# Linear attention in slots between the projection's tiles, in one decoder step

## The reference, cut to what matters

```
h = rmsnorm(x, norm1_g) * (1 + sc1) + sh1          # sc1, sh1, ... from c @ w_ada
q_a, k_a, v_a, g_lr, r_a, q_d, k_d, v_d = split_proj(h @ w_in)
log_a = log_sigmoid(g_lr @ w_gate_up + b_gate) / 16
# per token and head:  S_t = diag(exp(log_a_t)) S_{t-1} + k_t^T v_t ,  o_t = q_t S_t
# evaluated in chunks: b = cumsum(log_a) inside the chunk
att   = sum_k q * k * exp(b_t - b_s), causal
o     = att @ v + (q * exp(b)) @ S
S_new = exp(b_last) * S + (k * exp(b_last - b))^T @ v
o_a = rmsnorm(o, gla_norm_g) * silu(r_a)
# then: dilated softmax attention of q_d, k_d, v_d in 12 heads, output projection, MoE
```

## Time and profile before

| | us |
|---|---|
| runs, median (lowest to highest) | 1424.47 (1423.12 to 1428.05) |
| the profiled execution's own time | 1426.68 |
| its span, first to last instruction | 1425.1 |
| PE busy | 1141.1 (80%) |
| DVE busy | 699.1 (49%) |
| ACT busy | 579.0 (41%) |
| POOL busy | 127.0 (9%) |

### The profile page before, as it was taken

How to read it: one execution, slowest core, us unless ns; L and a number is a source line. 1 busy time by engine, 2 the same in 40 slices (tenths; PEclk the granted TensorE clock), 3 DMA queues, 4 the chain that set the end, 5 groups by cost and what they waited for, 6 DMA issues and landing times.

```text
span 1425.1 us, 18556 instructions
## 1 busy us (share of the span) xinstructions
PE 1141.1 (80%) x6899; PEld 639.2 (45%) x6900; DVE 699.1 (49%) x1029; ACT 579.0 (41%) x850; POOL 127.0 (9%) x135
## 2 busy tenths in 40 slices
PE   3799579549898989898779995029899999999810
PEld 0355256436566666665444453014445544444400
DVE  2434334344435454544733335428765686656557
ACT  2222324133535353535531113027755566555433
POOL 0000001000000000000010000522111111111032
PEclk9899789759999999999798998559999999999955
DMA  9763200062313232383142440068977797779255
GB/s 344 282 227 142 54 0 0 9 167 55 100 49 90 60 90 60 90 295 103 47 121 68 140 163 31 0 236 321 381 267 261 290 373 276 284 257 368 103 189 182
DMA packets 122341, 234.43 MB, mean 164 GB/s; under 512 B 11079, under 2 KB 54569, under 8 KB 119200
## 3 DMA queue, kind: packets, MB, share of 16 engines
q1 hardware_dynamic: 111760, 200.37, 41.3%
q0 software_dynamic: 7200, 21.06, 4.0%
q10 hardware_dynamic: 3312, 12.06, 2.1%
HBM read 197.60 MB, written 35.64 MB: 164 GB/s over the span
## 4 chain that ended last, share of the span: by engine, by line
PE 63%; DVE 13%; DMA 10%; ACT 5%; issue 5%; POOL 2%; SPq 1%; DVEq 0%; POOLq 0%; ACTq 0%
PE banks L1576 7%; PE banks L1577 6%; PE banks L1578 6%; PE banks L1915 5%; PE banks L1917 5%; PE banks L1916 5%; PE banks L1737 3%; DMA arena<-in_moe_w_gate_dram 3%; PE banks L1751 2%; PE banks L1765 2%; DVE arena L1237 2%; PE banks L1934 2%; PE banks L1936 2%; PE banks L1935 2%; PE banks L1856 2%
## 5 line engine op out<-in xcount | busy, mean ns | idle before, releaser
L1469 DVE SCALAR_TENSOR_TENSOR arena<-arena 128x2048 f16<-128x2048 f32 x96 | 217.5, 2287 | 80.8 <-ACT arena L959 80.7
L959 ACT ACTIVATE arena<-arena 128x2048 f16<-128x2048 f32 x96 | 180.5, 1907 | 92.7 <-DMA arena<-in_moe_w_up_dram 53.8
L1576 PE MATMUL banks<-arena 128*128 128x384 f16 (+5 forms) x576 | 191.5, 332 | 16.1 <-DVE arena L1119 12.4
L1577 PE MATMUL banks<-arena 128*128 128x384 f16 (+5 forms) x576 | 190.9, 331 | 0.0
L1578 PE MATMUL banks<-arena 128*128 128x384 f16 (+5 forms) x576 | 190.7, 331 | 0.0
L1915 PE MATMUL banks<-arena 128*128 128x512 f16 x368 | 141.0, 383 | 9.8 <-DVE arena L1482 9.8
L1917 PE MATMUL banks<-arena 128*128 128x512 f16 x368 | 140.7, 382 | 0.0
L1916 PE MATMUL banks<-arena 128*128 128x512 f16 x368 | 140.6, 382 | 0.0
L854 ACT ACTIVATE arena<-banks 128x512 f32<-128x512 f32 (+3 forms) x96 | 49.3, 514 | 129.9 <-PE banks L1751 129.9
L1237 DVE CUSTOM_DVE_ANT_0 arena<-banks,arena 128x128 f32<-128x128 f32 (+7 forms) x96 | 72.3, 753 | 46.0 <-PE banks L1737 45.8
L846 ACT ACTIVATE arena<-arena 128x128 f32<-128x128 f32 (+7 forms) x96 | 74.3, 774 | 28.3 <-DVE arena L1240 27.2
(11 more groups left out here) (325 smaller groups left out, 1694.1 us busy)
## 6 DMA issues: line engine op xcount, KB each, us to landing
arena<-in_moe_w_gate_dram SPq DMA_DIRECT2D x32, 1024.0 KB, 8.6
arena<-in_moe_w_up_dram SPq DMA_DIRECT2D x32, 1024.0 KB, 8.3
arena<-in_moe_w_down_dram SPq DMA_DIRECT2D x32, 1024.0 KB, 6.5
arena<-in_w_ada_dram SPq DMA_DIRECT2D x24, 1024.0 KB, 7.5
slot_rows<-arena ACTq DMA_DIRECT2D x23, 512.0 KB, 6.8
out_dram<-arena SPq DMA_DIRECT2D x20, 512.0 KB, 2.6
arena<-in_w_in_dram SPq DMA_DIRECT2D x18, 512.0 KB, 7.0
arena<-in_x_prompt_dram SPq DMA_DIRECT2D x16, 512.0 KB, 8.6
```

The lines of the kernel that those rows point to most:

```text
L959: A(w_hi[s][p // 2][:, (p % 2) * PIECE:(p % 2 + 1) * PIECE], stage[g % RING], ACT.Copy, scale=WS).then_inc(phi_ok, 1)
L1469: v.scalar_tensor_tensor(out=w_lo[s][p // 2][:, part], in0=stage[(PIECES * s + p) % RING], scalar=WS, in1=w_hi[s][p // 2][:, part], op0=AL ...
L1576: mm(out, hTh[:, k, tok], wh(k), start=(first and k == ks[0]), stop=False)
L1577: mm(out, hTh[:, k, tok], wl(k), start=False, stop=False)
```

## The change

Stage 1 is gone as a stage: its work is spread over the loop of stage 0, and the later stages are numbered one lower.

- The loop over tiles: while tile t is projected, PE does two "slots" for earlier tiles. The first slot (between the projection's halves) transposes the gate of tile t-1, forms the running sums of tile t-2, and the scores and the state's increment of tile t-3. The second slot (after the second half) makes the gate's product of t-1, three transposes for t-2 and the output of t-3. ACT and DVE do their part for one tile at a time (`after_b`, `after_a`) instead of for all at once.
- The slots need PSUM, so the projection keeps one pair of banks (4 and 5) and waits for its own stores before the next tile. The conditioning slices have three buffers in place of four.
- Two more steps finish the last chunks. `project_first` is now filled in there and between the steps of the sample tokens' state: t = 0 to 3 in the last two steps, 4 to 8 after them.
- silu(r) is one ACT instruction; the norm weight is multiplied into it rather than into the output; squares and their sums are made per tile.
- The weights of the first pair are loaded behind the last transposed tile, those of the second pair behind the last tile's projection, ahead of the barrier.
- On ACT the next tile's sum of squares (`rms`) stands ahead of `high_hT`; on DVE `norm` stands behind the store of the projection.

The diff, cut to its core (numbers of stages, renamed buffers and assertions are left out):

```diff
-        wa = [V(o_r + s * 2 * D, 2 * D) for s in range(4)]
+        wa = [V(o_r + s * 2 * D, 2 * D) for s in range(SLICES)]      # SLICES = 3
...
@@ SP
-            for n in range(4):
+            for n in range(3):
                 load_slice(n)
             load_ba(0)
...
-            stage_end(sp, 0)
...
+            sp.wait_ge(hT_ps, NT)
             load_w(0, w0)
+            sp.wait_ge(gproj_ps, NT)
+            sp.wait_ge(wP_in, 48)
+            load_w(1, wP)
+            move_rows(2)
...
             for hh in range(2):
                 load_strip(0, hh)
-            load_w(1, wP)
@@ ACT
+            def keep_out(c):
+                src = bank(7, 256) if c < PT else bank(7, 256, NB)
+                A(oG[0:rows_of(c), c], src, ACT.Copy).then_inc(og_cp, 1)
+                act.wait_ge(og_cp, c + 1)
+                if c >= 1:
+                    act.wait_ge(ossq_ok, c)
+                A(osq, oG[:, c], ACT.Square).then_inc(osq_ok, 1)
+            def gate_log(c):
...
+                lk.done(A(t1, z, ACT.Abs))
+                lk.done(A(t1, t1, ACT.Exp, scale=-1.0))
+                A(t1, t1, ACT.Ln, bias=C("one", rows_of(c))).then_inc(lnz_ok, 1)
+            def after_b(i):
+                act.wait_ge(gB_ps, i - 1)
+                if 0 <= i - 3 < PT:
+                    A(k2T, bank(3)[:, 3 * P:4 * P], ACT.Copy).then_inc(k2T_ok, 1)
+                if 0 <= i - 2 <= PT:
+                    gate_log(i - 2)
+                if 0 <= i - 4 < PT:
+                    keep_out(i - 4)
+            def after_a(i):
+                act.wait_ge(gA_ps, i)
+                if 0 <= i - 3 < PT:
+                    A(attS, bank(7), ACT.Copy).then_inc(att_cp, 1)
+                if 0 <= i - 2 < PT:
+                    A(E[0], bank(6, P), ACT.Exp).then_inc(edec_ok, 1)
...
             for t in range(NT):
                 n = rows_of(t)
+                if t >= 2:
+                    after_b(t)
+                if t + 2 < NT:
+                    rms(t + 2)
                 if t + 1 < NT:
                     high_hT(t + 1)
-                if t + 2 < NT:
-                    rms(t + 2)
+                if t >= 2:
+                    after_a(t)
                 act.wait_ge(gproj_ps, t + 1)
-                A(proj[0:n, t, 0:512], bank(4 + 2 * (t % 2), 512, n), ACT.Copy, scale=1.0 / WS).then_inc(gprojA, 1)
-            stage_end(act, 0)
+                A(proj[0:n, t, 0:512], bank(4, 512, n), ACT.Copy, scale=1.0 / WS).then_inc(gprojA, 1)
             act.wait_ge(wP_in, 48)
             for j in range(2):
                 split_high_part(j, w0, w0h)
...
+            A(rG, rG, ACT.Silu).then_inc(rsilu_ok, 1)
@@ DVE
+            def after_b(i):
+                dve.wait_ge(gB_ps, i - 1)
+                if 0 <= i - 3 < PT:
+                    lk.done(v.tensor_copy(q4T, bank(6, P)), wait=False)
+                    for h in range(HA):
+                        lk.done(v.tensor_copy(blkq[32 * h:32 * h + 32, P * h:P * h + P],
+                                              banks[32 * h:32 * h + 32, 3072 + P:3072 + 2 * P]), wait=False)
...
@@ PE
             def project_gla(t, j):
-                n, b = rows_of(t), 4 + 2 * (t % 2)
+                n, b = rows_of(t), 4
                 if j == 0:
                     pe.wait_ge(hT_ok, t + 1)
-                    if t >= 2:
-                        pe.wait_ge(gprojA, t - 1)
-                        pe.wait_ge(gprojB, t - 1)
+                    if t >= 1:
+                        pe.wait_ge(gprojA, t)
+                        pe.wait_ge(gprojB, t)
...
+            def first_slot(i):
+                if i >= 2:
+                    pe.wait_ge(loga_ok, i - 1)
+                if 0 <= i - 1 <= PT:
...
+                    last = tr(bank(3, n, RANK), proj[0:n, c, 512:528], ident[0:n, 0:n])
+                if 0 <= i - 2 < PT:
...
+                    for j, name in enumerate(("cum_mid", "cum_rest", "cum")):
+                        mm(bank(6)[:, j * P:(j + 1) * P], C(name), L, start=True, stop=True)
+                    last = mm(bank(6)[:, 3 * P:3 * P + 1], L, C("ones")[:, 0:1], start=True, stop=True)
+                if 0 <= i - 3 < PT:
...
+                    mm(bank(7), k2T, blkq, start=True, stop=True)
+                    last = mm(bank(3)[:, P:P + 256], E[2], proj[:, c, 256:512], start=True, stop=True)
+                last.then_inc(gA_ps, 1)
+            def second_slot(i):
...
+                last.then_inc(gB_ps, 1)
...
             for t in range(NT):
                 project_gla(t, 0)
...
                     turn_x(t + 1)
+                if t >= 1:
+                    first_slot(t)
                 project_gla(t, 1)
+                if t >= 1:
+                    second_slot(t)
                 if 2 * t + 1 < 16:
                     ada_slice(KC + 2 * t + 1)
-            stage_end(pe, 0)
...
+            for i in (NT, NT + 1):
+                project_first(2 * (i - NT))
+                first_slot(i)
+                project_first(2 * (i - NT) + 1)
+                second_slot(i)
```

More of the change, by code:

```diff
@@ L458, in _ @@
             sp.dma_start(gbc, norm1_g[0:1, :].partition_broadcast(P)).then_inc(ba_in, 16)
-            for n in range(4, 8):
+            for n in range(3, 8):
                 load_slice(n)
@@ L779, in _ @@
                 split_high_part(j, w0, w0h)
-            act.wait_ge(gate_ps, 2)
-            z = banks[:, 0:D]
-            lk.done(A(T1, z, ACT.Abs))
-            lk.done(A(sT1, bank(2, P, NB), ACT.Abs))
-            lk.done(A(T1, T1, ACT.Exp, scale=-1.0))
-            lk.done(A(sT1, sT1, ACT.Exp, scale=-1.0))
-            lk.done(A(T1, T1, ACT.Ln, bias=C("one")))
-            A(sT1, sT1, ACT.Ln, bias=C("one", NB)).then_inc(lnz_ok, 1)
-            act.wait_ge(gate_ps, 3)
-            ed = Steps(act, edec_ok)
@@ new lines, in _ @@
+            store_qkv(0, 0, 4)
+            after_a(NT)
+            store_qkv(0, 1, 5)
+            after_b(NT + 1)
+            store_qkv(0, 2, 4)
+            after_a(NT + 1)
+            act.wait_ge(loga_ok, NT)
+            A(sA, sL, ACT.Exp).then_inc(edec_ok, 1)
+            act.wait_ge(gprojB, NT)
+            A(rG, rG, ACT.Silu).then_inc(rsilu_ok, 1)
+            store_qkv(0, 3, 5)
+            after_b(NT + 2)
+            store_qkv(0, 4, 4)
+            act.wait_ge(ossq_ok, PT)
+            A(rs[:, 0:PT * HA], ss[:, 0:PT * HA], ACT.Sqrt, scale=1.0 / DV, bias=eps).then_inc(ostd_ok, 1)
@@ L828, in _ @@
+            store_qkv(0, 5, 5)
+            act.wait_ge(gend_ps, 3)
+            keep_out(PT)
+            store_qkv(0, 6, 4)
+            act.wait_ge(ossq_ok, NT)
+            A(rs[:, PT * HA:], ss[:, PT * HA:], ACT.Sqrt, scale=1.0 / DV, bias=eps).then_inc(ostd_ok, 1)
             act.wait_ge(gend_ps, 4)
@@ L1111, in _ @@
-            lk.done(v.memset(state[0], 0.0), wait=False)
-            dve.wait_ge(vec_in, 80)
-            for rows in (slice(0, NB), slice(32, 33)):
-                sc = mod[rows, SC2 * D:SC2 * D + D]
-                lk.done(v.scalar_tensor_tensor(out=sc, in0=sc, scalar=1.0, in1=nrm[rows], op0=ALU.add, op1=ALU.mult), wait=False)
-            def split_low_part(j, w, high, low):
-                k = slice(4 * j, 4 * j + 4)
-                v.scalar_tensor_tensor(out=low[:, k].rearrange("p k n -> p (k n)"), in0=w[:, k].rearrange("p k g n -> p (k g n)"),
-                                       scalar=WS, in1=high[:, k].rearrange("p k n -> p (k n)"), op0=ALU.mult,
-                                       op1=ALU.subtract).then_inc(wlo_ok, 1)
@@ L1178, in _ @@
+            for i in (NT, NT + 1):
+                after_b(i)
+                after_a(i)
+            dve.wait_ge(mod_in, 128 * GROUPS)
+            dve.wait_ge(vec_in, 80)
+            for rows in (slice(0, NB), slice(32, 33)):
+                m = mod[rows, SC2 * D:SC2 * D + D]
+                lk.done(v.scalar_tensor_tensor(out=m, in0=m, scalar=1.0, in1=nrm[rows], op0=ALU.add, op1=ALU.mult), wait=False)
             dve.wait_ge(gend_ps, 1)
-            v.tensor_copy(sc3, bank(0, 3 * NB)).then_inc(sc3_ok, 1)
+            v.tensor_copy(sc3, bank(6, 3 * NB)).then_inc(sc3_ok, 1)
```

494 lines of the change are left out of this document (240 added, 254 removed).

## The result

The changed kernel takes 1364.77 us (median of 4 runs, 1362.02 to 1368.9); the kernel before, on the same chip, 1426.26 us (the three runs named at the start and a fourth of 1429.38). The ratio is 0.9567, 95% interval 0.954 to 0.9594. The profiled execution took 1366.18 us, with a span of 1364.6. The forecast was 1361 us.

What follows compares the result with a forecast made beforehand. PE was taken to bound the steps: its terms summed to 187.9 us against 243.9, 56.0 less; with 8 us from the next stage's start, 64.0 less, giving a 1361 us median, range 1350 to 1372 (66%).

Steps and rivals of the forecast that it cites:

- (a): Projection loop on PE: keeps its nine projections, sixteen slices and eight transposed tiles, 98.8 us.
- (b): The slots on PE: 2.4 us for the first, 1.9 for the second; eight chunks with the sample rows' gate, 34.8 us.
- What must keep up: ACT's two runs per 15.6 us full step fit beside PE's work, by 0.6 and 1.0 us.
- (c): End of the loop: PE waits 3.7 us for the first pair's weight split, plus 3 us at lower clock: 6.7 us.
- (d): Nine tiles of the first pair's projection on PE, 3.9 us each: 35.1 us.
- (f): Ahead of the loop: with three buffers slice 7 is issued only after slice 4, 2 us later (bounds 0 and 3).
- (e): Sample state and ends on PE: 10.5 us, with the 16 instructions at 3.6 us (bound 7.2).
- The next stage: Start behind the barrier: weights already there, so transposes, ACT pass, high and low part take 6.3 to 8.0 us, against 15.0.
- Silu: Takes operations from ACT and DVE in the chunk loop, where PE lacked work for only 0.6 us: gain nothing.
- ACT as the bound of the steps: Rival in the loop's steps: ACT's runs too long, some 2.3 us lost per step, 1372 to 1395 us; 21%.
- the fall of the clock inside the loop: Rival: nine steps at half clock, +133 us, 1494, slower than before; 4%.
- more come back than counted: Rival: no clock loss at the wait, no delay ahead of the loop, faster next stage, better slot overlap: 1349 us; 8%.

## Why the prediction was right

The gain came from where it was looked for, and nearly as large: 64.0 us forecast, 60.5 in the span and 61.5 in the medians. That the whole came so close is in part luck, since the time behind the barrier, which the prediction left as it was, differs by up to 14 us between traces of one program; the stretch and the steps are the better test. By its steps:

- (a), (b): right. PE without a gap, 15.55 us a full step against 15.6, clock 1.00. The rates of single products from one chunk carried over to the slots.
- What must keep up: right, with more room than counted, 1.24 us for 0.6. Two squares a step on top changed nothing; eight cost what the sum of the rooms says, and the clock.
- (c): right. 3.35 us of waiting for 3.7, and 3 us of clock behind it; moving the split took back 6.2 of the 6.7.
- (d): right. 3.90 us a tile for 3.9.
- (f): right in its cause: slice 7 waits for slice 4, and that for the bias products. 2.66 us for 2: slice 7 begins 2.00 us later, and its 0.86 us at half clock behind the wait were not counted. In the nine traces with the same program ahead of the loop, the loop starts between 55.48 and 57.55.
- (e): mis-sized. The 16 instructions were taken at 3.6 us, and the bound of 7.2 was put on the same instructions. They took 4.1, but the fall of the clock went on over the products behind them, 3.3 us together. This and 0.7 us of the start are most of the 4.5 us by which the barrier is later than 53.6 + 187.9 = 241.5. Where the fall did not come, the stretch measured 185.54 us, against 185.9 of the sum without (f).
- The next stage: right, 6.4 us within 6.3 to 8.0, and the chain is the one named. Behind it 5.9 us run at 0.57.
- Silu, costed at nothing: right for the sum; but the reason given, that it takes work from a place where PE never waited, says too little. At its new place the old form cost 4.9 us of the stretch against the first trace, 9.2 against one without the fall of the clock.

Of the rivals, ACT as the bound of the steps is refuted, and so is the fall of the clock inside the loop: it was 0.99 there, with the fp32 products of the slots among the others. What the earlier trace rows warned of did come, but at the same 16 instructions as there. Nor did more come back than counted: the clock was lost at the wait, the loop started later, and the next stage's first products ran at 0.57.

No run takes the slots themselves out of the loop. That most of the gain is theirs is read from the two traces, in the waits of PE that are gone; the runs show singly what the fill, the early load, the split, the order ahead of the loop and the short silu are worth.

## What to carry to other kernels

In this kernel, work of short dependent steps could be hidden in slots of a PE-bound loop at the price of its PE time alone, since each handover had its time beside other PE work; count the runs of each helper engine between two slots, and not its share of the step. A wait of PE is to be priced with the clock behind it: the waits of 20.6 and 11.0 us that the runs provoked cost 31 and 15.6, the 3.35 us that one run removed gave 6.2. And where a load, a split or a product only has to be earlier, look for the idle stretch of its engine before the stage's end: three such moves took the ratio from 0.9567 to 0.9482, another 12 us, and the second pair's first product from 252.42 to 240.26 us.

## What the runs showed of the hardware

- Behind 16 fp32 instructions with 8 rows the clock fell to half in eight traces of the same sequence (10.97 us up to the 64 in seven, 9.34 in one) and stayed at 1.00 in two (7.65 us), with PE busy throughout in all ten; what differs is open.
- A change on PE between an fp16 product of 384 columns and an fp32 product of 256 columns with 8 rows cost 0.13 us in the mean of both directions, 2.1 us over 16 changes.
- Each of the three table loads of a full step takes 1.28 us, and the next instruction begins 0.01 to 0.02 us later.
